# A three-product float32 matmul on one NeuronCore: the high weights times both parts of the input in one product of 512 columns, the two halves added by VectorE

## The chip, the cores and the metric

The kernel runs on one NeuronCore of a Trainium2 chip. The metric is the device time of one execution in microseconds (us). A kernel is timed in several runs, and the median is its time.

## What is computed

Two residual networks are run one behind the other on 256 tokens of 2,048 features. The first has two layers that mix a gated unit over chunks with grouped attention, over the tokens and over 256 context tokens; in its last layer the context is only needed for keys and values. The second has four mixers, each followed by a layer norm: a state-space mixer with a causal convolution ("ssd"), attention with forget gates ("fox"), attention with latent queries and keys ("mla"), and a diagonal recurrence with a gate behind it ("s5"). Cut to what matters, each of them is projections around something small:

```python
proj = h @ w_in[layer]                       # 2,048 x 5,632, first network
x = x + gate * (concat([sgu, attn]) @ w_out[layer])
...
z, xbc, dt = split(h @ ssd_w_in)             # 2,048 x 10,368, then y @ ssd_w_out (4,096 x 2,048)
q, k, v, z, f = split(h @ fox_w_in)          # 2,048 x 8,320,  then y @ fox_w_out
q_lat, kv_lat, k_pe, z = split(h @ mla_w_in) # 2,048 x 3,200,  then two up-projections and y @ mla_w_out
u, z = split(h @ s5_w_in)                    # then y @ s5_w_glu, a sigmoid, and @ s5_w_out
h = layer_norm(ALPHA * h + out)              # behind each mixer of the second network
```

All inputs and the output are float32.

## The kernel before, in words

**Data.** Features lie on the 128 partitions and tokens along the free axis: `xT` is 16 tiles of 128 features by 256 tokens. All weights come as one stream of units of 8 tiles of 128 x 128 (512 KB), in an order that `sequence()` fixes. SyncE loads unit n into `raw[n % 4]` once unit n - 4 has been multiplied (semaphore `multiplied`).

**Precision.** A weight and an input are each kept as two parts in the matmul's reduced float32 type. For a unit of weights ScalarE makes the high part, `w_hi` = a rounded copy of `raw` (`split_hi`, L452), and VectorE the low part, `w_lo` = `raw` - `w_hi` (`split_lo`, L459). For the input of a projection the same is done once, into `act_hi` and `act_lo`. A weight tile then takes three products: `w_hi` x `act_hi` (L513), `w_hi` x `act_lo` (L515) and `w_lo` x `act_hi` (L517), all summed in one PSUM bank. Each product is preceded by its own load of the weights.

**Blocks and slots.** `flow` runs one stage. Its work is a list of blocks; a block is 128 output features, mostly 16 weight tiles (2 units) and so 48 products. In the first network's layer 0 a block has 512 columns (tokens and context), and so have the four blocks of keys and values of layer 1, in two pieces of 256; all others have 256. When all tiles of a block are multiplied, it is taken out of its bank: by ScalarE (an activation, its line is that of a `take_...` function) for the projections into a mixer and for the gate of s5, by VectorE for those out of it (`add_gated` L1651, `add_scaled` L1692: the result goes onto `xT`).

**Order on the engines.** There is no scheduler; each engine runs through the slots g in order. In slot g

- TensorE multiplies block g and then does the mixer's own products that stand in that slot (`tensor_side`: transposes, scores, sums);
- ScalarE makes the high parts up to two units beyond the end of block g (`split_hi(ends[g] + 1 + AHEAD)`, `AHEAD` = 2), does the mixer's steps of the slot (`scalar_early`), waits until block g is multiplied and takes it;
- VectorE makes the low parts up to the same unit, does the mixer's steps of the slot (`vector_side`), and takes block g only if it is a block that VectorE takes.

```python
def scalar(act):
    for g in range(slots):
        split_hi(act, ends[g] + 1 + AHEAD)
        ...
        if taken_by(g, "act"):
            act.wait_ge(multiplied, ends[g] + 1)
            blocks[g].take(act, blocks[g].bank).then_inc(taken["act"], 1)
```

So the high part of the third unit behind block g comes after block g was taken, while the low part of that unit waits for that high part alone.

**Stages.** In this order: the modulation of the first network, the projections into and out of layer 0 and layer 1, ssd in and out, fox in and out, mla in and out, s5 in, the gate of s5, s5 out, the last layer norm. The ssd projections come in eight groups; from the second group on a group has ten blocks, b, c, four x and four z (`ssd_order`). On VectorE a b, c or x block brings three convolution steps in the slot behind it (`add_taps`, L1926), and the group brings a reciprocal, gates, scalings and masks (L1954 to L1996). `norm_root` is a scratch tile of 128 x 256, used by the norms at stage starts.

## Time and profile before

| | us |
|---|---|
| median of 3 runs | 3648.49 |
| lowest and highest | 3647.06, 3650.87 |
| the profiled execution: its own time | 3651.35 |
| the profiled execution: span, first to last instruction | 3649.5 |
| busy: PE, DVE, ACT, POOL | 3413.2, 1960.7, 1845.3, 438.4 |

PE is TensorE, PEld its weight loads, DVE VectorE, ACT ScalarE, POOL GpSimd, SP SyncE. "L459" is line 459 of the kernel before. In a timeline each row has its start in us, its length in us, the engine, the line, the operation, the tiles (out<-in), partitions x elements and, with x, how many were merged; in brackets stands how long the engine was idle before it and what ended that. Busy PE time counts overlapping matmuls as one; how fast matmuls follow each other is read from their starts. The granted clock of TensorE was 0.970 of full speed on average.

### The profile page before, as it was taken

The page shows a single profiled execution, that of the slowest core. Times are in us where ns is not written, and L with a number is a line of the kernel's source. Part 1 is how long each engine was busy: PE and PEld are TensorE (multiplying, and loading weights), DVE is VectorE, ACT ScalarE, POOL GpSimd, SP SyncE. Part 2 cuts the span into 40 slices and gives each one's busy share as a digit, 9 for nine tenths or more (in the row PEclk, how much of TensorE's full clock was granted, in tenths as well). Part 3 has the DMA queues.
Part 4 walks back from the last instruction along what each step waited for, and adds up shares of the span by engine and source line. Part 5 has one row for each costly group of instructions (what it writes and reads, how often), then busy time and mean ns, then how long its engine had stood idle before and what let it go on. Part 6 is the DMA issues. An engine that isn't in the chain of part 4 may idle for free.

```text
span 3649.5 us, 60172 instructions
## 1 busy us (share of the span) xinstructions
PE 3413.2 (94%) x25589; PEld 3067.3 (84%) x25589; DVE 1960.7 (54%) x2698; ACT 1845.3 (51%) x2906; POOL 438.4 (12%) x604
## 2 busy tenths in 40 slices
PE   6899999999899999999999989999989998898897
PEld 2577767778688999999999979999989988788797
DVE  1423322233554455666666465555576556899755
ACT  1334433332456645677675344555455654666443
POOL 0110011101000000000000010000020003787302
PEclk9999999999999999999999989999989999899998
DMA  9654555532233455554554535455544334333353
GB/s 386 216 174 150 173 174 192 196 116 98 75 122 133 168 179 179 177 177 168 193 178 158 183 133 180 168 168 169 169 138 162 129 135 165 116 126 117 114 177 136
DMA packets 157963, 589.83 MB, mean 162 GB/s; under 512 B 18352, under 2 KB 18384, under 8 KB 156032
## 3 DMA queue, kind: packets, MB, share of 16 engines
q1 hardware_dynamic: 135216, 497.64, 39.7%
q0 software_dynamic: 21904, 86.24, 6.8%
q8 instruction: 203, 3.33, 0.4%
q10 hardware_dynamic: 576, 2.10, 0.2%
q14 instruction: 64, 0.52, 0.0%
HBM read 583.69 MB, written 2.21 MB: 161 GB/s over the span
## 4 chain that ended last, share of the span: by engine, by line
PE 75%; DVE 10%; DMA 6%; ACT 5%; issue 3%; POOL 1%; POOLq 0%; DVEq 0%; SPq 0%; ACTq 0%
PE psum_all L513 21%; PE psum_all L517 21%; PE psum_all L515 21%; DMA raw<-in_stream 4%; DMA mod_early<-in_stream 2%; DVE w_lo L459 2%; PE psum_all L725 2%; ACT w_hi L452 1%; DVE s_vd L2906 1%; PE psum_all L1327 1%; PE psum_all L1297 1%; DVE s_vb L2905 1%; ACT ssd_seg L1866 1%; DVE s_im_n L2912 1%; DVE s_im_c L2915 1%
## 5 line engine op out<-in xcount | busy, mean ns | idle before, releaser
L513 PE MATMUL psum_all<-act_hi,w_hi 128*128 128x256 f32 (+1 forms) x6704 | 2059.0, 307 | 85.0 <-DVE act_lo L884 55.5
L515 PE MATMUL psum_all<-act_lo,w_hi 128*128 128x256 f32 (+1 forms) x6704 | 2021.7, 302 | 0.0
L517 PE MATMUL psum_all<-act_hi,w_lo 128*128 128x256 f32 (+1 forms) x6704 | 2020.6, 301 | 0.0
L459 DVE TENSOR_TENSOR w_lo<-raw,w_hi 128x1024 fp32r<-128x1024 f32 x866 | 1070.2, 1244 | 1259.4 <-ACT w_hi L452 1257.4
L513 PEld LDWEIGHTS psum_all<-act_hi,w_hi 128*128 128x128 f32 x6704 | 1296.4, 193 | 182.7 <-issue 101.0
L452 ACT ACTIVATE w_hi<-raw 128x1024 fp32r<-128x1024 f32 x866 | 910.3, 1057 | 849.5 <-DMA raw<-in_stream 848.1
L515 PEld LDWEIGHTS psum_all<-act_lo,w_hi 128*128 128x128 f32 x6704 | 1297.2, 193 | 42.2 <-issue 3.1
L517 PEld LDWEIGHTS psum_all<-act_hi,w_lo 128*128 128x128 f32 x6704 | 1295.4, 193 | 41.7
L699 POOL DMA_DIRECT2D mod_late<-in_stream x128 | 67.7, 533 | 657.5 <-PE psum_all L725 554.9
L952 POOL TENSOR_TENSOR ln_acc<-xT 128x256 f32<-128x256 f32 x8 | 5.9, 735 | 1028.7 <-DVE xT L1692 1028.7
L644 PE MATMUL psum_all<-mod_early,s_silu 128*32 128x512 f32 x256 | 57.8, 645 | 29.0 <-DMA mod_early<-in_stream 28.8
L952 POOL TENSOR_TENSOR ln_acc<-ln_acc,xT 128x256 f32<-128x256 f32 x44 | 47.4, 1077 | 215.0 <-DVE xT L1692 215.0
L1926 DVE SCALAR_TENSOR_TENSOR conv_acc<-conv_x,params,conv_acc 128x255 f32<-128x255 f32 x144 | 69.3, 481 | 3.4
L644 PEld LDWEIGHTS psum_all<-mod_early,s_silu 128*32 128x32 f32 x256 | 9.2, 112 | 72.8 <-DMA mod_early<-in_stream 68.5
L725 PE MATMUL psum_all<-mod_late,small 128*2 128x512 f32 x512 | 67.4, 599 | 0.0
L1651 DVE SCALAR_TENSOR_TENSOR xT<-psum_all,modulation,xT 128x256 f32<-128x256 f32 x32 | 15.4, 482 | 85.2 <-PE psum_all L517 85.1
L1866 ACT ACTIVATE ssd_seg<-ssd_seg,ssd_src 128x128 f32<-128x128 f32 x192 | 58.5, 388 | 2.0 <-DMA ssd_seg<-acs_rows 2.0
L2001 POOL DMA_DIRECT2D acs_rows<-ssd_acs x1 | 0.6, 560 | 480.7 <-DVE ssd_red L1918 480.7
L669 DVE TENSOR_TENSOR modulation<-psum_all,params 128x16 f32<-128x16 f32 x12 | 2.1, 175 | 102.9 <-PE psum_all L660 60.7
L2006 POOL DMA_DIRECT2D ssd_seg<-acs_rows x8 | 4.3, 534 | 437.0 <-PE psum_all L1810 435.2
L980 DVE TENSOR_TENSOR ln_d<-xT,ln_half 128x256 f32<-128x256 f32 (+1 forms) x28 | 43.4, 1548 | 12.4 <-POOLq L441 12.3
L866 ACT ACTIVATE xT<-xT,params 128x256 f32<-128x256 f32 x64 | 34.8, 592 | 29.8 <-DVE xT L1013 28.8
(475 smaller groups left out, 3325.5 us busy)
## 6 DMA issues: line engine op xcount, KB each, us to landing
raw<-in_stream SPq DMA_DIRECT2D x866, 512.0 KB, 3.2
mod_late<-in_stream POOLq DMA_DIRECT2D x128, 512.0 KB, 5.0
mod_early<-in_stream SPq DMA_DIRECT2D x64, 512.0 KB, 8.9
ssd_seg<-acs_rows POOLq DMA_DIRECT2D x8, 1536.0 KB, 6.7
ctxT<-in_ctx SPq DMA_DIRECT2D x2, 2048.0 KB, 13.9
xT<-in_x SPq DMA_DIRECT2D x1, 2048.0 KB, 16.0
fox_key_cum<-cum_rows POOLq DMA_DIRECT2D x1, 2048.0 KB, 8.3
out<-xT SPq DMA_DIRECT2D x4, 512.0 KB, 2.6
```

Of the source, the lines that this page charges most:

```text
L452: act.activation(w_hi[:, n % RING, :], raw[:, n % RING, :], ACT.Copy).then_inc(hi_ready, 1)
L459: dve.tensor_tensor(w_lo[:, n % RING, :], raw[:, n % RING, :], w_hi[:, n % RING, :].bitcast(F32), ALU.subtract).then_inc(lo_ready, 1)
L513: pe.matmul(sums, w_hi[:, n % RING, cols], block.rhs(kk, True, block.width), start=(kk == 0), stop=False)
L515: pe.matmul(sums, w_hi[:, n % RING, cols], block.rhs(kk, False, block.width), start=False, stop=False)
L517: last = pe.matmul(sums, w_lo[:, n % RING, cols], block.rhs(kk, True, block.width), start=False, stop=(kk == block.kt - 1))
L644: last = pe.matmul(bank[rows, :], s_of[:, k, :], units_of[:, m % ring, h * 512:(h + 1) * 512], start=(pair == 0), stop=(pair == PAIRS - 1))
L699: pool.dma_start(late_units[:, m % LATE_RING, :], ins["stream"][u]).then_inc(late_landed[m % LATE_RING], 16)
L725: last = pe.matmul(bank[rows, :], s_late[:, 2 * pair + e, :], late_units[:, m % LATE_RING, h * 512:(h + 1) * 512], start=(pair == 0), stop ...
L952: pool.tensor_tensor(acc, acc if b % 8 > 1 else xT[:, b - 1, :], xT[:, b, :], ALU.add) \
L980: dve.tensor_tensor(self.d[:, a:end, :], xT[:, a:end, :], self.half[:, :].unsqueeze(1).broadcast_to([P, end - a, T]), ALU.subtract) \
L1866: one = act.activation(s, s, ACT.Relu, bias=src_cum[:, g * HG + j, k:k + 1], scale=-1.0)
L1926: dve.scalar_tensor_tensor(out=conv_acc[i % 2][:, back:T], in0=conv_x[i % 2][:, 0:T - back], scalar=conv_col(block, tap), in1=conv_acc[i % ...
```

## The change

The two parts of the input become one tile, `act_parts`, part 0 high and part 1 low. A block may be `wide`: its high weights are then multiplied with both parts in one product of 512 columns (two pieces of 256) into the whole bank, high x high in columns 0 to 255 and high x low in columns 256 to 511; the low weights times the high input (256 columns) go to the first half as before. The halves are added on the way out. For a block that ScalarE takes, VectorE adds them into `norm_root` (`add_halves`, a sum over two), and ScalarE reads that tile in place of the bank; for a block that VectorE takes, a second operation adds the second half. A semaphore `halves_added` carries the first from VectorE to ScalarE, and an addition waits until ScalarE has taken the block before. Wide are: in layer 1 all blocks but those of keys and values, 40; in ssd in 81; in fox in 65; in mla in those whose input is the tokens, 25; in the gate of s5 16; and in the five stages out of a mixer (layer 1, ssd, fox, mla, s5) the blocks 0 to 14, 75 in all. Not wide are layer 0, the last block of every stage out, the up-projections of mla and s5 in. The order in which ssd's second input is kept in the tile changes with it (`result`), and its products take the same operands.

```diff
+HIGH, LOW, BOTH = 0, 1, slice(0, 2)
...
-        act_hi = keep("act_hi", [P, 32 * T], F32R)
-        act_lo = keep("act_lo", [P, 32 * T], F32R)
+        act_parts = keep("act_parts", [P, 2, 32 * T], F32R)
+        act_hi, act_lo = act_parts[:, 0, :], act_parts[:, 1, :]
...
+                    if item.wide and item.taker == "act":
+                        added_at[0] += 1
+                        item.added, item.previous, last_wide[0] = added_at[0], last_wide[0], item
...
-                block.bank = psum[place][:, 0:block.width]
+                block.bank, block.both = psum[place][:, 0:block.width], psum[place].rearrange("p (v t) -> p v t", v=2)
...
-                    pe.matmul(sums, w_hi[:, n % RING, cols], block.rhs(kk, True, block.width),
-                              start=(kk == 0), stop=False)
-                    pe.matmul(sums, w_hi[:, n % RING, cols], block.rhs(kk, False, block.width),
-                              start=False, stop=False)
-                    last = pe.matmul(sums, w_lo[:, n % RING, cols], block.rhs(kk, True, block.width),
+                    if block.wide:
+                        pe.matmul(block.both, w_hi[:, n % RING, cols], block.rhs(kk, BOTH, block.width),
+                                  start=(kk == 0), stop=False)
+                    else:
+                        pe.matmul(sums, w_hi[:, n % RING, cols], block.rhs(kk, HIGH, block.width),
+                                  start=(kk == 0), stop=False)
+                        pe.matmul(sums, w_hi[:, n % RING, cols], block.rhs(kk, LOW, block.width),
+                                  start=False, stop=False)
+                    last = pe.matmul(sums, w_lo[:, n % RING, cols], block.rhs(kk, HIGH, block.width),
                                      start=False, stop=(kk == block.kt - 1))
...
+            def add_halves(dve, block, end):
+                dve.wait_ge(multiplied, end)
+                if block.previous:
+                    dve.wait_ge(taken["act"], block.previous.count)
+                dve.reduce_sum(norm_root[:, :], block.both.rearrange("p v t -> p t v"), AX_X).then_inc(halves_added, 1)
...
                     if taken_by(g, "act"):
-                        act.wait_ge(multiplied, ends[g] + 1)
-                        blocks[g].take(act, blocks[g].bank).then_inc(taken["act"], 1)
+                        if blocks[g].wide:
+                            act.wait_ge(halves_added, blocks[g].added)
+                        else:
+                            act.wait_ge(multiplied, ends[g] + 1)
+                        blocks[g].take(act, norm_root[:, :] if blocks[g].wide else blocks[g].bank).then_inc(taken["act"], 1)
...
+                    if taken_by(g, "act") and blocks[g].wide:
+                        add_halves(dve, blocks[g], ends[g] + 1)
                     if taken_by(g, "dve"):
                         dve.wait_ge(multiplied, ends[g] + 1)
-                        blocks[g].take(dve, blocks[g].bank).then_inc(taken["dve"], 1)
+                        blocks[g].take(dve, blocks[g].both if blocks[g].wide else blocks[g].bank).then_inc(taken["dve"], 1)
...
         def add_scaled(dve, ps, b):
-
-            return dve.scalar_tensor_tensor(out=xT[:, b, :], in0=xT[:, b, :], scalar=ALPHA, in1=ps,
-                                            op0=ALU.mult, op1=ALU.add)
+            if b == KT - 1:
+                return dve.scalar_tensor_tensor(out=xT[:, b, :], in0=xT[:, b, :], scalar=ALPHA, in1=ps,
+                                                op0=ALU.mult, op1=ALU.add)
+            ordered = order["vector"]
+            dve.scalar_tensor_tensor(out=xT[:, b, :], in0=xT[:, b, :], scalar=ALPHA, in1=ps[:, 0, :],
+                                     op0=ALU.mult, op1=ALU.add).then_inc(ordered.sem, 1)
+            dve.wait_ge(ordered.sem, ordered.step())
+            return dve.tensor_tensor(xT[:, b, :], xT[:, b, :], ps[:, 1, :], ALU.add)
```

`add_gated` gets the same second operation as `add_scaled` for the last layer, and the other calls pass `wide=True` for the blocks listed.

**TensorE, in the middle of fox in**, the last two weight tiles of a block and the score product of a head behind it. Before:

```order
L515 MATMUL psum_all<-act_lo,w_hi 128x256
L517 MATMUL psum_all<-act_hi,w_lo 128x256
L513 MATMUL psum_all<-act_hi,w_hi 128x256
L515 MATMUL psum_all<-act_lo,w_hi 128x256
L517 MATMUL psum_all<-act_hi,w_lo 128x256
L2082 MATMUL psum_all<-consts,fox_p_19718 128x128 x3
L2219 MATMUL psum_all<-fox_k,fox_q 128x128
```

Now:

```order
L533 MATMUL psum_all<-act_parts,w_lo 128x256
L526 MATMUL psum_all<-act_parts,w_hi 128x512
L533 MATMUL psum_all<-act_parts,w_lo 128x256
L2130 MATMUL psum_all<-consts,fox_p_17483 128x128 x3
L2267 MATMUL psum_all<-fox_k,fox_q 128x128
```

(L2082, now L2130, turns the probabilities of the head before.) Two products are one, of 512 columns, and the third is as it was. This occurs 5,072 times.

**VectorE, in ssd in**, the slots of the first two x blocks of a group (`add_taps` of the block before, the reciprocal and scalings of the group before, its low part). Before:

```order
L1926 SCALAR_TENSOR_TENSOR conv_acc_11085<-conv_x_11087,params,conv_acc_11085 128x253
L1985 RECIPROCAL ssd_root<-ssd_root 128x256
L1990 SCALAR_TENSOR_TENSOR ssd_z_11075<-ssd_z_11075,params,ssd_root 128x256 x4
L459 TENSOR_TENSOR w_lo<-raw,w_hi 128x1024 x2
L1926 SCALAR_TENSOR_TENSOR conv_acc_11084<-conv_x_11086,params,conv_acc_11084 128x255
L1926 SCALAR_TENSOR_TENSOR conv_acc_11084<-conv_x_11086,params,conv_acc_11084 128x254
L1926 SCALAR_TENSOR_TENSOR conv_acc_11084<-conv_x_11086,params,conv_acc_11084 128x253
L1996 TENSOR_TENSOR act_lo<-ssd_z_11075,act_hi 128x1024
L459 TENSOR_TENSOR w_lo<-raw,w_hi 128x1024 x2
L1926 SCALAR_TENSOR_TENSOR conv_acc_11085<-conv_x_11087,params,conv_acc_11085 128x255
L1926 SCALAR_TENSOR_TENSOR conv_acc_11085<-conv_x_11087,params,conv_acc_11085 128x254
```

Now:

```order
L1972 SCALAR_TENSOR_TENSOR conv_acc_10353<-conv_x_10355,params,conv_acc_10353 128x253
L2031 RECIPROCAL ssd_root<-ssd_root 128x256
L2036 SCALAR_TENSOR_TENSOR ssd_z_10344<-ssd_z_10344,params,ssd_root 128x256 x4
L561 TENSOR_REDUCE norm_root<-psum_all 128x256
L468 TENSOR_TENSOR w_lo<-raw,w_hi 128x1024 x2
L1972 SCALAR_TENSOR_TENSOR conv_acc_10352<-conv_x_10354,params,conv_acc_10352 128x255
L1972 SCALAR_TENSOR_TENSOR conv_acc_10352<-conv_x_10354,params,conv_acc_10352 128x254
L1972 SCALAR_TENSOR_TENSOR conv_acc_10352<-conv_x_10354,params,conv_acc_10352 128x253
L2042 TENSOR_TENSOR act_parts<-ssd_z_10344,act_parts 128x1024
L561 TENSOR_REDUCE norm_root<-psum_all 128x256
L468 TENSOR_TENSOR w_lo<-raw,w_hi 128x1024 x2
L1972 SCALAR_TENSOR_TENSOR conv_acc_10353<-conv_x_10355,params,conv_acc_10353 128x255
```

An addition out of the bank (`norm_root<-psum_all`) stands at the end of each slot, behind the slot's own work and ahead of the next two low parts.

**ScalarE, in the same stage**, the slots of the first two z blocks of a group. Before:

```order
L1866 ACTIVATE ssd_seg<-ssd_seg,ssd_src 128x128 x6
L2024 ACT_TABLE_LOAD
L2024 ACTIVATE ssd_z_11075<-psum_all 128x256
L452 ACTIVATE w_hi<-raw 128x1024 x2
L1857 ACTIVATE ssd_x<-conv_acc_11085 128x256
L1872 ACT_TABLE_LOAD
L1872 ACTIVATE ssd_seg<-ssd_seg 128x1536
L2024 ACT_TABLE_LOAD
L2024 ACTIVATE ssd_z_11075<-psum_all 128x256
L452 ACTIVATE w_hi<-raw 128x1024 x2
```

Now:

```order
L1912 ACTIVATE ssd_seg<-ssd_seg,ssd_src 128x128 x6
L2070 ACT_TABLE_LOAD
L2070 ACTIVATE ssd_z_10343<-norm_root 128x256
L461 ACTIVATE w_hi<-raw 128x1024 x2
L1903 ACTIVATE ssd_x<-conv_acc_10353 128x256
L1918 ACT_TABLE_LOAD
L1918 ACTIVATE ssd_seg<-ssd_seg 128x1536
L2070 ACT_TABLE_LOAD
L2070 ACTIVATE ssd_z_10343<-norm_root 128x256
L461 ACTIVATE w_hi<-raw 128x1024 x2
```

The order is the same, and the two high parts (`w_hi<-raw`) of the next slot come behind a take as before; the take now reads `norm_root`, which VectorE has written in that slot.

## Rows read from the trace of the kernel before

**Rows 1.** The page, part 5: busy us, mean ns, idle before, what ended it
```profile
L459 DVE TENSOR_TENSOR w_lo<-raw,w_hi 128x1024 fp32r<-128x1024 f32 x866 | 1070.2, 1244 | 1259.4 <-ACT w_hi L452 1257.4
```

**Rows 2.** Waits of PE in the whole span: us in total, times, longest
```profile
PE psum_all L513 <- DVE w_lo L459: 13.7, 4, 6.3
PE psum_all L1818 <- ACT ssd_x L1857: 16.3, 8, 2.8
```

**Rows 3.** Timeline of PE, products of 256 columns: start, us, instruction
```profile
1251.20 0.28 PE L513 MATMUL psum_all<-act_hi,w_hi 128*128 128x256 f32 x1
...
1251.92 0.28 PE L513 MATMUL psum_all<-act_hi,w_hi 128*128 128x256 f32 x1
```

**Rows 4.** Timeline of PE, layer 1, products of 512 columns in two pieces
```profile
985.43 0.39 PE L513 MATMUL psum_all<-act_hi,w_hi 128*128 128x512 f32 x1
...
991.55 0.39 PE L513 MATMUL psum_all<-act_hi,w_hi 128*128 128x512 f32 x1
```

**Rows 5.** Groups of VectorE by shape: busy us, mean ns, idle before
```profile
L1692 DVE SCALAR_TENSOR_TENSOR xT<-xT,psum_all 128x256 f32<-128x256 f32 x64 | 26.6, 416 | 10.9 <-PE psum_all L517 10.2
...
L1507 DVE TENSOR_REDUCE head_stat<-psum_all 128x1 f32<-128x512 f32 x32 | 20.5, 685 | 2.1 <-PE psum_all L1299 1.9
```

**Rows 6.** Busy us by stretch: PE, PEld, DVE, ACT, POOL, then clock and DMA
```profile
1741.80:1807.90 66.10, 64.33 (x533) 62.93 (x532) 44.34 (x57) 48.46 (x80) 0.53 (x1) 1.00 0.54 183
2255.00:2299.00 44.00, 44.00 (x364) 43.69 (x363) 23.95 (x39) 23.15 (x38) 0.00 (x0) 1.00 0.50 168
1268.60:1309.30 40.70, 40.70 (x342) 40.70 (x342) 22.56 (x30) 21.07 (x32) 0.00 (x0) 1.00 0.54 182
3441.00:3527.50 86.50, 86.50 (x723) 86.50 (x722) 51.24 (x72) 41.62 (x59) 0.00 (x0) 1.00 0.54 183
2710.00:2750.00 40.00, 39.38 (x315) 38.97 (x314) 32.71 (x74) 25.16 (x38) 0.00 (x0) 0.98 0.50 167
```

**Rows 7.** Timeline of ScalarE: a block is taken, six groups of ten blocks apart
```profile
1537.05 0.56 ACT L2015 ACTIVATE conv_acc<-psum_all,params 128x256 f32<-128x256 f32 x1 [4.66 <-PE psum_all L517]
...
1944.08 0.39 ACT L2024 ACTIVATE ssd_z<-psum_all 128x256 f32<-128x256 f32 x1 [4.46 <-PE psum_all L517]
```

**Rows 8.** Timeline of VectorE in a group of ten blocks
```profile
1754.02 1.52 DVE L1926 SCALAR_TENSOR_TENSOR conv_acc<-conv_x,params,conv_acc 128x255 f32<-128x255 f32 x3
...
1790.99 2.36 DVE L459 TENSOR_TENSOR w_lo<-raw,w_hi 128x1024 fp32r<-128x1024 f32 x2 [2.33 <-ACT w_hi L452]
1793.27 0.42 DVE L1954 TENSOR_TENSOR ssd_z<-ssd_z,ssd_y 128x256 f32<-128x256 f32 x1
```

**Rows 9.** Timeline of ScalarE in the same group
```profile
1754.84 0.56 ACT L2015 ACTIVATE conv_acc<-psum_all,params 128x256 f32<-128x256 f32 x1
...
1755.55 1.06 ACT L452 ACTIVATE w_hi<-raw 128x1024 fp32r<-128x1024 f32 x1
...
1774.59 2.17 ACT L452 ACTIVATE w_hi<-raw 128x1024 fp32r<-128x1024 f32 x2
...
1782.94 0.38 ACT L2024 ACTIVATE ssd_z<-psum_all 128x256 f32<-128x256 f32 x1
1783.22 1.99 ACT L452 ACTIVATE w_hi<-raw 128x1024 fp32r<-128x1024 f32 x2
...
1789.91 2.00 ACT L452 ACTIVATE w_hi<-raw 128x1024 fp32r<-128x1024 f32 x2
```

**Rows 10.** Timelines in the gate of s5: a take on ScalarE, a step on VectorE
```profile
3500.18 0.46 ACT L3026 ACTIVATE s_glu<-psum_all,params 128x256 f32<-128x256 f32 x1
3500.54 1.05 ACT L452 ACTIVATE w_hi<-raw 128x1024 fp32r<-128x1024 f32 x1
...
3500.31 0.42 DVE L2942 TENSOR_TENSOR act_lo<-s_glu,act_hi 128x256 fp32r<-128x256 f32 x1 [0.48 <-ACT act_hi L2864]
```

**Rows 11.** Timeline of VectorE at the start of two stages
```profile
1427.63 2.35 DVE L459 TENSOR_TENSOR w_lo<-raw,w_hi 128x1024 fp32r<-128x1024 f32 x2
...
2199.39 3.46 DVE L459 TENSOR_TENSOR w_lo<-raw,w_hi 128x1024 fp32r<-128x1024 f32 x3
```

More of the change, by code:

```diff
@@ L307 @@
     shape: Any = None
+    wide: bool = False
+    added: int = 0
+    previous: Any = None
 @dataclass
@@ L1649, in take @@
                         dve.wait_ge(ctx_landed, 16)
+                    if last and b < KT - 1:
+                        ordered = order["vector"]
+                        for n in range(2):
+                            one = dve.scalar_tensor_tensor(out=xT[:, b, :], in0=ps[:, n, :],
+                                                           scalar=mod_col(layer, b + 2 * KT, 0), in1=xT[:, b, :],
+                                                           op0=ALU.mult, op1=ALU.add)
+                            if n == 0:
+                                one.then_inc(ordered.sem, 1)
+                                dve.wait_ge(ordered.sem, ordered.step())
+                        return one
                     for n, x in enumerate((xT, ctxT)[:parts]):
@@ L2174, in output_blocks @@
                 return [Block(KT, T, act_rhs(T, first=KT), lambda dve, ps, b=b: add_scaled(dve, ps, b), "dve",
-                              None if b else wait_tile) for b in range(KT)]
+                              None if b else wait_tile, wide=b < KT - 1) for b in range(KT)]
         def keys(tile):
@@ L2322, in fox @@
                 take = take_f if name == "f" else take_z(h) if name == "z" else take_part(parts[name], h)
-                blocks.append(Block(KT, T, act_rhs(T), take, wait=None if blocks else norms[0].wait_tile))
+                blocks.append(Block(KT, T, act_rhs(T), take, wait=None if blocks else norms[0].wait_tile, wide=True))
             blocks = halves_first(blocks, lead) + heads.output_blocks()
@@ L3036, in s5 @@
             blocks += [None]
-            blocks += [Block(KT, T, act_rhs(T, first=KT), take_glu(b), wait=None if b else wait_y) for b in range(KT)]
+            blocks += [Block(KT, T, act_rhs(T, first=KT), take_glu(b), wait=None if b else wait_y, wide=True) for b in range(KT)]
             blocks += [Block(KT, T, act_rhs(T), lambda dve, ps, b=b: add_scaled(dve, ps, b), "dve",
-                             None if b else wait_out) for b in range(KT)]
+                             None if b else wait_out, wide=b < KT - 1) for b in range(KT)]
             norms.append(LayerNorm(3, 4, 5, out=False))
```

51 lines of the change are left out of this document (31 added, 20 removed).

## Prediction

> **What bounds the kernel now.** I began with the busy times: TensorE is busy for 94% of the span, VectorE for 54%, ScalarE for 51%. Such a share is an average, so the waits came next: TensorE waits for low weight parts for 13.7 us in all and for the transposed inputs of ssd for 16.3 us [rows 2]. In nearly every stretch it is the bound. Then its timeline, for the price of a product: six of 256 columns take 1251.92 - 1251.20 = 0.72 us, 0.120 each [rows 3]; 27 of 512 columns, their columns in two pieces of 256 as the change has them, take 6.12 us, 0.2267 each [rows 4]. So two narrow products cost 0.240 and the wide one 0.2267: each product seems to carry about 13 ns besides its columns.
>
> Last, and for this change above all, the two engines that prepare weights. VectorE's low parts leave it idle for 1259.4 us, 1257.4 of these until ScalarE's high part is there [rows 1]. That idle time is the lead of ScalarE over nobody: VectorE is a follower with time to spare. In a group of ten ssd blocks it is busy for 44.3 of 66.1 us, in two heads of fox for 23.95 of 44.0, in fifteen gate blocks for 51.2 of 86.5, at the start of mla for 32.7 of 40.0 [rows 6].
>
> **The change, part by part.**
>
> *TensorE.* A weight tile costs 3 x 0.120 = 0.360 us today and 0.2267 + 0.120 = 0.3467 then: 0.0133 less. Tiles by stage: layer 1 in 40 x 16 = 640, out of the mixers 60 x 16 + 15 x 32 = 1,440, ssd in 1,296, fox in 1,040, mla in 400, the gate 256; in sum 5,072 and 67 us. It counts only where TensorE stays the bound.
>
> The Trainium skill ("TensorE: Matmul & The Clock Gate", Part 1, "Wait — 56ns, not 53.3ns?") puts the fixed cost of a product at full clock at about 2.5 ns. By that the 5,072 removed products would be worth 13 us and not 67. The trace differs: 13 ns per product stand in rows 3 and 4, and the sum goes by them.
>
> *The addition.* VectorE gets 227 sums of two halves out of PSUM. None is in the trace. The nearest row is the reduction of 512 columns out of PSUM, 0.685 us; the lower bound is an operation on 256 columns of PSUM, 0.416 [rows 5]. The upper one, if the jumps between the halves cost a second pass over 512 columns, is 0.685 plus twice the 0.27 by which these two differ, 1.22. I take 0.69, since as many elements are read. For the 75 blocks that VectorE takes, a second operation of 0.42 us is added; VectorE has no more than this to do there, nobody takes the bank sooner than 5.5 us later, and only the last norms see a trace of it: 1 us in all.
>
> *The wait it adds.* Today VectorE's work of a slot and ScalarE's take are independent. Now the take stands behind the addition, the addition behind VectorE's work of the slot, and that behind the low parts of the two units ahead; and behind the take stand ScalarE's next high parts, for which VectorE's next low parts wait. This is a ring, and one turn of it is one block. In it VectorE is idle from the end of its addition to the first low part: 0.04 until ScalarE starts, 0.71 until ScalarE has taken a convolution block and starts a high part (1754.84 to 1755.55) or 0.28 for a z block (1782.94 to 1783.22), and 1.08 until the low part starts (1789.91 to 1790.99) [rows 8, 9]. That is 1.83 or 1.40 us. A stretch can't be shorter than VectorE's own work in it, plus 0.69 and this handover per block.
>
> - *ssd in*, ten blocks: 44.3 + 10 x 0.69 + 6 x 1.83 + 4 x 1.40 = 67.8. In one slot ScalarE is the slower: from a high part at 1774.59 to the take at 1782.94 are 8.35 us, where VectorE needs 1.08 + 2.28 for the pair of low parts + 1.5 for the convolution steps + 0.73 = 5.6 [rows 8, 9]: 2.8 more, 70.6. TensorE's wait for the transposes' inputs, 16.3 / 8 = 2.0 per group today [rows 2], stays, since its release comes from ScalarE in that same stretch: 72.5. Today it is 66.1 [rows 6], and 407.0 / 6 = 67.8 on average over six groups [rows 7]. The difference is 6.4 or 4.7; I take 5.5, so six groups cost 33. The group before them has TensorE's side work of two groups; 3. The end of the stage, 1.
> - *Starts of ssd and fox.* VectorE ends a long chain of small steps and then makes low parts that ScalarE has readied long before (1427.63 and 2199.39 [rows 11]). Now the addition, the take and one high part come first, 0.69 + 0.04 + 0.71 + 1.08 = 2.5, plus 0.7 for the first block's own addition: 3 for fox, and 6 for ssd, whose next block is caught too.
> - *mla's start*: 32.7 + 7 x (0.69 + 1.40) = 47.3 against 40.0 [rows 6]: 7.3 slower. The other 17 wide blocks give back 17 x 16 x 0.0133 = 3.6. Net 3.7.
> - *The gate of s5*: 51.2 + 15 x (0.69 + 0.04 + 0.36 + 1.08) = 83.8, and 0.48 per block for which VectorE waits inside its slot for ScalarE's high part of the input [rows 10]: 91.0 against 86.5 [rows 6]. 4.5 slower, and nothing gained.
> - *fox in*: 23.95 + 7 x 2.09 = 38.6, below 44.0 - 1.5 [rows 6]. The ring is not the bound, and TensorE's gain counts in full: 1,040 x 0.0133 = 13.8. The same holds for layer 1 in, 8.5, whose slots have little work on VectorE, and in the stages out, where ScalarE does not wait: 19.2.
>
> *Sum:* - 8.5 - 19.2 - 13.8 + 33 + 3 + 1 + 6 + 3 + 3.7 + 4.5 + 1 = + 13.7 us. The profiled execution took 3651.35 us, so 3665; the median lies 2.9 lower, so the forecast is **3662 us**. With the clock a little worse or better and the ssd group at its two ends the case itself spans 3645 to 3685. A run of this kernel can tell about 0.2% (7.3 us) from no change.
>
> **Rivals.**
>
> - *The additions are covered.* VectorE is idle for over 1,200 us, and the additions are worth 157. If the lead of two units absorbs the longer path to the take, no stretch becomes longer; this decides if an ssd group comes out at 66 us or less. Then all 67.5 us are gained less the starts (9) and the norms (1): 3651 - 57 - 3 = 3591. For it: ScalarE's high parts also wait for transfers today. Against it: the bound above is a sum over a ring, and a lead does not shorten a ring. 0.10.
> - *The ring binds, but barely.* With additions of 0.42 an ssd group has 67.8 + 2.8 - 2.7 = 67.9 and no further wait: no loss in six groups, mla's start + 5.4, the gate + 0.5: - 41.5 + 10 + 1.8 + 0.5 + 1 = - 28, 3620. 0.13.
> - *The addition is slow.* At 1.22, each turn of a binding ring is 0.53 longer: 70 ssd blocks, 7 of mla, 15 of the gate, 49 us: 3711. 0.09.
> - *The wide product gains nothing.* If the 13 ns come from something that a row of 512 and 256 columns in turn keeps, such as the change between loads of different parts ahead of each product, the 41.5 us of the stages where TensorE is the bound are not gained, and the rest stays: 3662 + 41.5 = 3703. The 0.2267 of rows 4, with a load of its own for each product, speaks against it. 0.03. (By the Trainium skill's 2.5 ns, "TensorE: Matmul & The Clock Gate", 41.5 x 2.5 / 13.3 = 7.8 us of them would remain, and the time would be 3696.)
> - *More of the span at the low clock.* The granted clock is 1.00 in the group of rows 6 and falls where TensorE idles; it will idle for some 9 us more per ssd group. Where the ring binds, a slower product is hidden in it, so I give this no term of its own and let it stand in the upper half of the range.
>
> **How the numbers follow.** The forecast has 0.62, the rivals 0.10, 0.13, 0.09 and 0.03, and 0.03 is left for what I don't see. Faster by over 0.2% (below 3641): 0.10 + 0.13 + 0.02 = 0.25. Within 0.2%: the lower part of the forecast's own range, 0.15. Slower: 0.60. The range is 3615 to 3705: it takes in the barely binding ring and most of what lies above the forecast, and leaves out the covered case and the slow addition, 0.19.
>
> **What would show it.** In the profile after, products of 512 columns should follow one of 256 by 0.120 and be followed after 0.227. The addition should take 0.69. An ssd group should last 71 to 73 us, with VectorE's idle time put down to high parts in pieces of about 1.8 and 1.4 us, and TensorE waiting for low parts for tens of us where today it is 13.7 in all. The fox stretch of 44.0 should last 42.5, fifteen gate blocks about 91. If an ssd group lasts 66 us or less, the argument of the ring is wrong; if fox in isn't about 10 us shorter, the price of the product is.

## The result, and the profile after

| | us |
|---|---|
| before, median of 4 runs | 3647.77 (3644.67 to 3650.87) |
| after, median of 4 runs | 3699.22 (3693.91 to 3713.11) |
| ratio after to before | 1.0145, 95% interval 1.0128 to 1.0162 |
| after, the profiled execution: its own time, its span | 3694.71, 3692.9 |

The change makes the kernel 51 us slower by the medians, and 43.4 by the two profiled executions (3694.71 - 3651.35). Forecast were 13.7. The time lies in the predicted range of 3615 to 3705, on the side that was forecast, but far up in it. The medians are known to a few us only (four runs each, 3693.91 to 3713.11 after), and all that follows by stage is read from one trace of each kernel.

The first view is the timeline of TensorE in layer 1 (start, us, instruction), the answer to [rows 3, 4]:

```profile
1249.72 0.40 PE L526 MATMUL psum_all<-act_parts,w_hi 128*128 128x512 f32 x1
1249.95 0.28 PE L533 MATMUL psum_all<-act_parts,w_lo 128*128 128x256 f32 x1
1250.07 0.40 PE L526 MATMUL psum_all<-act_parts,w_hi 128*128 128x512 f32 x1
...
1252.19 0.40 PE L526 MATMUL psum_all<-act_parts,w_hi 128*128 128x512 f32 x1
```

From 1249.72 to 1252.19 there are seven weight tiles: 0.353 each, where the sum of [rows 3] and [rows 4] promised 0.3467 and before had 0.360. Half of the gain per tile isn't there. The other half of the bill is on VectorE and ScalarE. Groups of VectorE (busy us, mean ns, idle before, what ended it), the answer to [rows 1]:

```profile
L468 DVE TENSOR_TENSOR w_lo<-raw,w_hi 128x1024 fp32r<-128x1024 f32 x866 | 1066.4, 1247 | 1109.9 <-ACT w_hi L461 1108.6
L561 DVE TENSOR_REDUCE norm_root<-psum_all 128x256 f32<-128x512 f32 x227 | 155.7, 686 | 29.3 <-PE psum_all L533 28.1
```

The addition takes 0.686, as forecast, and VectorE still idles for over 1,100 us. But its consumer waits. Waits of TensorE and of ScalarE (us in total, times, longest), the answer to [rows 2]:

```profile
PE psum_all L526 <- DVE w_lo L468: 31.1, 21, 9.5
PE psum_all L1871 <- ACT ssd_c L1903: 29.3, 7, 5.1
PE psum_all L1864 <- ACT ssd_x L1903: 20.4, 8, 3.4
```

```profile
ACT conv_acc L2061 <- DVE norm_root L561: 125.9, 46, 9.9
ACT ssd_z L2070 <- DVE norm_root L561: 61.7, 18, 5.3
```

The last two rows are new: 188 us in which ScalarE stands before a take of ssd until VectorE has added the halves. Before, it stood 62 us at the same takes, until TensorE had multiplied the block:

```profile
ACT conv_acc L2015 <- PE psum_all L517: 41.1, 16, 5.3
ACT ssd_z L2024 <- PE psum_all L517: 21.3, 15, 4.5
```

TensorE's waits for low parts rise from 13.7 to 31.1, and it now waits for the inputs that ScalarE makes from the taken blocks more than before: ssd_c 29.3 and ssd_x 20.4, where it was 3.5 and 16.3.

One turn of the ring of an ssd block, VectorE first and then ScalarE:

```profile
1565.66 0.68 DVE L561 TENSOR_REDUCE norm_root<-psum_all 128x256 f32<-128x512 f32 x1
1568.27 2.36 DVE L468 TENSOR_TENSOR w_lo<-raw,w_hi 128x1024 fp32r<-128x1024 f32 x2 [1.93 <-ACT w_hi L461]
1570.54 1.52 DVE L1972 SCALAR_TENSOR_TENSOR conv_acc<-conv_x,params,conv_acc 128x255 f32<-128x255 f32 x3
1571.98 0.55 DVE L2027 TENSOR_TENSOR ssd_cb<-psum_all,consts 128x384 f32<-128x384 f32 x1
1572.45 0.68 DVE L561 TENSOR_REDUCE norm_root<-psum_all 128x256 f32<-128x512 f32 x1
```

```profile
1566.38 0.60 ACT L2061 ACTIVATE conv_acc<-norm_root,params 128x256 f32<-128x256 f32 x1 [1.98 <-DVE norm_root L561]
1566.88 0.40 ACT L2063 ACTIVATE conv_x<-norm_root 128x256 f32<-128x256 f32 x1
1567.19 2.00 ACT L461 ACTIVATE w_hi<-raw 128x1024 fp32r<-128x1024 f32 x2
```

The addition ends at 1566.34, ScalarE takes at 1566.38 and makes a high part at 1567.19, and VectorE's low parts start at 1568.27: a handover of 1.93 in which VectorE does nothing. The forecast had 1.83. The turn lasts 6.79 us, while TensorE needs 16 x 0.353 = 5.65 for the block, besides the mixer's own products. The same kind of take ten blocks apart, at ScalarE:

```profile
1541.90 0.60 ACT L2061 ACTIVATE conv_acc<-norm_root,params 128x256 f32<-128x256 f32 x1 [5.43 <-DVE norm_root L561]
...
1615.69 0.60 ACT L2061 ACTIVATE conv_acc<-norm_root,params 128x256 f32<-128x256 f32 x1 [5.34 <-DVE norm_root L561]
```

This group takes 73.8 us, and the four behind it, by the same take, 73.2 to 75.0. Forecast were 72.5, the average of before was 67.8 [rows 7]. Stretches with busy us of PE, PEld, DVE, ACT and POOL, then granted clock, DMA share and GB/s: all of ssd in, the start of mla, the two heads of fox, the gate [rows 6]:

```profile
1401.40:2006.50 605.10, 537.72 (x3007) 459.36 (x3007) 407.48 (x552) 389.73 (x643) 4.82 (x9) 0.94 0.48 162
...
2739.40:2794.10 54.70, 44.14 (x218) 36.70 (x217) 39.08 (x81) 25.71 (x39) 0.00 (x0) 0.91 0.38 125
2294.98:2338.25 43.27, 43.27 (x251) 37.78 (x251) 28.21 (x46) 23.33 (x37) 0.00 (x0) 1.00 0.52 170
3477.60:3568.50 90.90, 86.93 (x481) 73.05 (x479) 58.89 (x87) 42.20 (x59) 0.00 (x0) 1.00 0.52 174
```

VectorE's two rows within ssd in show that the ring is closed there (busy us, mean ns, idle before):

```profile
L468 DVE TENSOR_TENSOR w_lo<-raw,w_hi 128x1024 fp32r<-128x1024 f32 x163 | 194.2, 1223 | 179.8 <-ACT w_hi L461 179.7
...
L561 DVE TENSOR_REDUCE norm_root<-psum_all 128x256 f32<-128x512 f32 x80 | 54.7, 684 | 10.2 <-PE psum_all L533 10.0
```

Its work (407.5 us), its waits for ScalarE's high parts (179.7) and its waits for TensorE (10.0) make 597 of the 605 us: VectorE waits for ScalarE or works, and hardly ever waits for TensorE. What TensorE waits for in this stage are mostly ssd_c and ssd_x, 49.7 us; low parts are 14.1 (8.4 before). The loop holds TensorE up through the inputs of the mixer's own products, and not, as forecast, mainly through low parts.

And ssd in before, in the same view of stretches:

```profile
1403.20:1963.20 560.00, 528.62 (x4305) 516.37 (x4305) 360.97 (x473) 387.78 (x644) 4.83 (x9) 0.98 0.51 176
```

By stage, from the last product of the stage before to its own last one, in the profiled executions (us). The kernels on the right are those of the next section: no additions, wide only where unbound (so narrow in ssd in, mla in and the gate), the later take, the later take but not in layer 1.

| stage | before | after | forecast | measured | no add. | unbound | later | later 2 |
|---|---|---|---|---|---|---|---|---|
| layer 1 in | 357.9 | 356.9 | -8.5 | -1.0 | 356.4 | 356.5 | 393.6 | 358.2 |
| ssd in | 560.0 | 605.1 | +43 | +45.1 | 554.1 | 554.3 | 579.6 | 581.1 |
| fox in | 437.9 | 431.4 | -10.8 | -6.5 | 428.6 | 431.9 | 428.8 | 429.9 |
| mla in | 308.2 | 318.1 | +3.7 | +9.9 | 304.8 | 307.4 | 313.6 | 314.5 |
| the gate | 118.3 | 121.7 | +4.5 | +3.4 | 115.6 | 115.7 | 114.6 | 114.1 |
| five stages out | 566.9 | 562.1 | -18.2 | -4.8 | 552.5 | 555.1 | 557.8 | 557.3 |

Stages without a wide product and what lies behind the last stage moved by -2.8 in sum. Together that is the + 43.4, within rounding.

How far a stage scatters can be read from experiments 1 and 2, which are the changed kernel with rows of products behind its last stage. Ahead of these rows their traces give, beside the column "after": layer 1 in 355.1 and 355.5, ssd in 609.5 and 609.3, fox in 431.3 and 431.9, mla in 320.2 and 319.7, the gate 121.3 and 120.0, the stages out 556.7 and 560.3. Differences of 2 to 5 us in a stage show little.

### The profile page after: what moved, and what is told of

Read it like the earlier page. It is cut to its first block, busy times and chain, and to the rows that moved or that the text cites. A ratio compares the mean times of both kernels' runs of the same rounds, so it can differ in the third digit from the quotient of the medians.

```text
span 3692.9 us, 50550 instructions
## 1 busy us (share of the span) xinstructions
PE 3401.5 (92%) x20517; PEld 2807.4 (76%) x20517; DVE 2129.6 (58%) x3000; ACT 1846.6 (50%) x2906; POOL 448.9 (12%) x604
## 4 chain that ended last, share of the span: by engine, by line
PE 63%; DVE 16%; ACT 9%; DMA 6%; issue 4%; POOL 1%; POOLq 0%; DVEq 0%; SPq 0%; ACTq 0%
PE psum_all L526 21%; PE psum_all L533 17%; PE psum_all L529 7%; PE psum_all L531 7%; DVE w_lo L468 5%; DMA raw<-in_stream 4%; ACT w_hi L461 4%; DMA mod_early<-in_stream 2%; PE psum_all L752 2%; DVE norm_root L561 1%; PE psum_all L1324 1%; PE psum_all L1354 1%; DVE s_vd L2954 1%; DVE s_im_n L2960 1%; DVE s_vb L2953 1%
## 5 line engine op out<-in xcount | busy, mean ns | idle before, releaser
L533 PE MATMUL psum_all<-act_parts,w_lo 128*128 128x256 f32 (+1 forms) x6704 | 2015.0, 301 | 0.0
L526 PE MATMUL psum_all<-act_parts,w_hi 128*128 128x512 f32 x5072 | 1846.6, 407 | 64.3 <-DVE w_lo L468 31.1
L533 PEld LDWEIGHTS psum_all<-act_parts,w_lo 128*128 128x128 f32 x6704 | 1290.4, 192 | 45.5 <-issue 2.9
L461 ACT ACTIVATE w_hi<-raw 128x1024 fp32r<-128x1024 f32 x866 | 899.1, 1052 | 621.4 <-DMA raw<-in_stream 620.4
L526 PEld LDWEIGHTS psum_all<-act_parts,w_hi 128*128 128x128 f32 x5072 | 971.0, 191 | 312.6 <-issue 51.5
L529 PE MATMUL psum_all<-act_parts,w_hi 128*128 128x512 f32 (+1 forms) x1632 | 593.2, 363 | 40.2 <-DVE act_parts L911 32.6
L531 PE MATMUL psum_all<-act_parts,w_hi 128*128 128x512 f32 (+1 forms) x1632 | 577.3, 354 | 0.0
L529 PEld LDWEIGHTS psum_all<-act_parts,w_hi 128*128 128x128 f32 x1632 | 313.8, 192 | 127.7 <-issue 69.4
L531 PEld LDWEIGHTS psum_all<-act_parts,w_hi 128*128 128x128 f32 x1632 | 314.3, 193 | 38.4 <-issue 0.5
L561 DVE TENSOR_REDUCE norm_root<-psum_all 128x256 f32<-128x512 f32 x227 | 155.7, 686 | 29.3 <-PE psum_all L533 28.1
L2061 ACT ACTIVATE conv_acc<-norm_root,params 128x256 f32<-128x256 f32 x48 | 28.8, 601 | 125.9 <-DVE norm_root L561 125.9
```

Source lines behind the costliest of these rows:

```text
L461: act.activation(w_hi[:, n % RING, :], raw[:, n % RING, :], ACT.Copy).then_inc(hi_ready, 1)
L526: pe.matmul(block.both, w_hi[:, n % RING, cols], block.rhs(kk, BOTH, block.width), start=(kk == 0), stop=False)
L529: pe.matmul(sums, w_hi[:, n % RING, cols], block.rhs(kk, HIGH, block.width), start=(kk == 0), stop=False)
L531: pe.matmul(sums, w_hi[:, n % RING, cols], block.rhs(kk, LOW, block.width), start=False, stop=False)
L533: last = pe.matmul(sums, w_lo[:, n % RING, cols], block.rhs(kk, HIGH, block.width), start=False, stop=(kk == block.kt - 1))
L561: dve.reduce_sum(norm_root[:, :], block.both.rearrange("p v t -> p t v"), AX_X).then_inc(halves_added, 1)
```

## The experiments

Two explanations had to be told apart: the ring, which costs where it binds, and the price of the wide product, which gives less than it should everywhere. Each got a test that leaves the other alone. Every kernel was timed next to the kernel before, whose median was 3647.6 to 3650.2 us each time; a ratio is to that.

**1. The price by itself (e1_rows).** Behind the last stage, rows of products with a weight load each, whose results are used nowhere:

```
...
+            for t in range(64):
+                product(halves, hi(t), x(t, BOTH))
+                product(one[:, 0:T], lo(t), x(t))
...
```

and six others in the same manner.

> The kernel after, and behind its last stage seven rows of products, each with its own weight load, VectorE, ScalarE and the stream idle: three of 256 columns per tile; 512 in two pieces and 256 in turn (the change); 512 in one piece and 256; 512 in two pieces and 256 into another bank; 512 in two pieces alone; 512 in one piece alone; 512 in two pieces and twice 256. Start to start at full clock. In the changed kernel the pair takes 0.235 + 0.117 = 0.352 to 0.356 us, not 0.3467. Theory 'the mixed row keeps it': three of 256 take 0.360, the pair 0.352 to 0.356 here too, two pieces or one, and 512 alone 0.227 per product. Rival 'traffic of the other engines': the pair comes down to 0.347 or less here, where they are idle. Rival 'pieces': the row of one piece takes 0.347 and that of two pieces 0.354. Rival 'the same bank written twice running': only the row with another bank takes 0.347.

The timeline of TensorE. The pair in turn runs from the first row to the second (64 tiles), the one whose 512 columns are in one piece to the third, the one into another bank to the fourth, 128 products of 512 columns in two pieces alone to the fifth:

```profile
3734.82 0.40 PE L3112 MATMUL psum_all<-act_parts,w_hi 128*128 128x512 f32 x1
...
3757.43 0.40 PE L3112 MATMUL psum_all<-act_parts,w_hi 128*128 128x512 f32 x1
...
3780.05 0.40 PE L3112 MATMUL psum_all<-act_parts,w_hi 128*128 128x512 f32 x1
...
3802.66 0.40 PE L3112 MATMUL psum_all<-act_parts,w_hi 128*128 128x512 f32 x1
...
3831.70 0.39 PE L3112 MATMUL psum_all<-act_parts,w_hi 128*128 128x512 f32 x1
```

22.61 / 64 = 0.3533 per tile, and the same for the other two; 29.04 / 128 = 0.2269 for a product of 512 alone, 0.2267 once the row is under way, as in [rows 4]. Three products of 256 took 0.360 per tile. So neither the two pieces, nor the bank, nor the traffic of the other engines matters: all were idle here. A product of 512 and one of 256 in turn cost 0.0067 more than each in a row of its own.

The seventh row has one product of 512 and then two of 256 for each tile. From the start of its first tile to that of its last, 63 tiles later:

```profile
3860.71 0.39 PE L3112 MATMUL psum_all<-act_parts,w_hi 128*128 128x512 f32 x1
...
3890.14 0.39 PE L3112 MATMUL psum_all<-act_parts,w_hi 128*128 128x512 f32 x1
```

That is 29.43 / 63 = 0.467 per tile, and 0.2267 + 2 x 0.120 is 0.4667: here there is no extra. So the theory of the mixed row holds for one narrow product behind each wide one, as the change has it, and not for every row that mixes the two widths.

**2. Is it the change of width? (e5_rows_grouped)** The same rows, with 1, 2, 4 and 8 wide products running and then as many narrow ones.

> The kernel after with rows of products behind its last stage again. In the first such run a tile took 0.360 us in three products of 256, 0.3533 in 512 and 256 in turn, and 512 alone 0.2267 each: 0.0067 more than the sum of the two. Theory 'the change of width costs it': 1, 2, 4 and 8 wide products, then as many narrow ones, take 0.3533, 0.3500, 0.3483 and 0.3475 us per tile. Rival 'it comes with each product of low weights, or each change of its inputs': 0.3533 for all four. Further rows: 384 columns alone 0.120 + 128 x 0.4167 ns = 0.1733; 384 and 256 in turn 0.1733 + 0.120 + 0.003 to 0.007; 128 alone 0.067 if the fixed cost stays 13 ns; 512 and 128 in turn 0.293 and 0.007 to 0.020 if the extra grows with the difference in width.

Where runs of 2, of 4 and of 8 begin, and where the last ends:

```profile
3757.62 0.64 PE L3112 MATMUL psum_all<-act_parts,w_hi 128*128 128x512 f32 x2
...
3779.93 0.63 PE L3112 MATMUL psum_all<-act_parts,w_hi 128*128 128x512 f32 x2
...
3802.38 0.63 PE L3112 MATMUL psum_all<-act_parts,w_hi 128*128 128x512 f32 x2
...
3824.73 0.52 PE L3112 MATMUL psum_all<-act_parts,w_hi 128*128 128x384 f32 x2
```

Per tile 0.3486, 0.3508 and 0.3492 us, after 0.3533 in single turns. It falls, so the product of low weights isn't what costs; but it doesn't fall in the order expected (0.3500, 0.3483, 0.3475): runs of 4 are dearer than runs of 2. The extra per turn is 7, 4, 16 and 20 ns for 1, 2, 4 and 8. A fixed price per change of width is therefore wrong too, as the seventh row above had shown. The 384 columns took 0.1733, as expected, and 384 and 256 in turn 0.2933, the plain sum: no extra at all. A product of 128 took 0.112 and not 0.067; 512 and 128 in turn 0.340, 1.6 ns over the sum, where 7 to 20 were expected. What makes the extra of 512 and 256 in turn stays open.

**3. The ring taken away (e2_no_addition).**

```
-                    if taken_by(g, "act") and blocks[g].wide:
-                        add_halves(dve, blocks[g], ends[g] + 1)
...
+                        act.wait_ge(multiplied, ends[g] + 1)
+                        blocks[g].take(act, blocks[g].bank).then_inc(taken["act"], 1)
```

> Leaves out the 227 additions: ScalarE takes the first half of the bank, so the product of high weights and low inputs is not added in there. VectorE's 156 us of additions and ScalarE's wait for them go. Theory 'ring': ssd in, mla in and the gate, 45.1, 9.9 and 3.4 us longer than before, fall back to before's length or by up to 5, 1 and 1 us below it, so the whole takes 3628 to 3640. Rival 'the products themselves are slower there' (two pieces, the bank written twice, the layout of the parts): ssd in stays over 590 us and the whole over 3675.

3615.39 us, 0.9905 of before (0.9887 to 0.9924), 13 us below the expected range. ssd in takes 554.1 us, mla in 304.8, the gate 115.6, and the granted clock of ssd in is back at 0.97 without anything done for it:

```profile
1404.40:1958.40 554.00, 521.17 (x3008) 447.98 (x3009) 359.21 (x472) 388.47 (x643) 4.83 (x9) 0.97 0.53 177
```

So the low clock in the changed kernel comes with the additions and isn't a cause beside them; for the same products TensorE is busy 537.7 us with them and 521.2 without.

The run also measures what the wide products give in the whole kernel: 3649.09 - 3615.39 = 33.7 us, and 5,072 tiles x 0.00667 = 33.8. Where TensorE is the bound all through and at the full clock, it shows to the hundredth: the two heads of fox take 43.27 us and the fifteen gate blocks 84.8, where before 44.01 and 86.4 less 0.0067 per tile are 43.26 and 84.8. By stage the sum doesn't come out so well. In ssd in the price would be 8.6 us, and the stage takes 554.1, just what it takes with narrow products in the three kernels of experiment 8 (554.3, 553.5, 554.5). Why these are about 6 us shorter than the one trace of the kernel before isn't known, and so the agreement in the sum may in part be luck.

And the run gives what the additions cost in all: 3699.22 - 3615.39 = 84 us. The forecast's own terms say 13.7 + 67.5 = 81, but with a gain of 0.0133 per tile; with half of that, the gain given up in ssd in, mla in and the gate is 11.2 and not 22.4 us, and the same terms say 70. The 81 is near the 84 by luck.

**4. The ring made longer (e7_addition_twice).** Each addition of ssd in is made twice.

```
+                if block.place is not None:
+                    dve.reduce_sum(norm_root[:, :], block.both.rearrange("p v t -> p t v"), AX_X).then_inc(order["vector"].sem, 1)
+                    dve.wait_ge(order["vector"].sem, order["vector"].step())
                 dve.reduce_sum(norm_root[:, :], block.both.rearrange("p v t -> p t v"), AX_X).then_inc(halves_added, 1)
```

> The change, with each addition of ssd in made twice, one after the other (81 more of 0.69 us, 56 us of VectorE, which is idle for over 1,100). Theory 'ring': 70 of them lie in stretches where it binds, so ssd in becomes 70 x 0.69 = 48 us longer (40 to 56), 649, and the whole 3740 to 3755. Rival 'the loss is one of the low clock or of TensorE's own waits, the ring has slack': ssd in grows by less than 20 and the whole stays under 3720.

3737.15 us (ratio 1.0242, 1.0226 to 1.0258), 38 more than the change, and ssd in is 641.3 us, 36 longer. VectorE in ssd in, the added group and what is left of its idle time:

```profile
L468 DVE TENSOR_TENSOR w_lo<-raw,w_hi 128x1024 fp32r<-128x1024 f32 x161 | 191.1, 1222 | 160.7 <-ACT w_hi L461 160.7
...
L564 DVE TENSOR_REDUCE norm_root<-psum_all 128x256 f32<-128x512 f32 x80 | 55.3, 691 | 2.8
L562 DVE TENSOR_REDUCE norm_root<-psum_all 128x256 f32<-128x512 f32 x80 | 54.7, 683 | 9.2 <-PE psum_all L533 9.1
```

An engine that idles for 180 us in this stage is given 55 us more, and the stage grows by 36 (by 32 against the two other traces of the changed kernel, 609). If each addition counts in full where the ring binds, that is about 47 to 53 of the 80, not the 70 counted, and stage and whole end a little below what was expected. The rival, under 20 us, is out.

**5. The ring opened at ScalarE (e4_take_later).** ScalarE makes the high parts of the next slot first and takes the block behind them.

```
                 for g in range(slots):
                     split_hi(act, ends[g] + 1 + AHEAD)
+                    if g and taken_by(g - 1, "act") and blocks[g - 1].wide:
+                        take_wide(g - 1)
...
```

> All products and additions as in the change, but ScalarE takes a wide block only after the high parts of the next slot, so that these no longer stand behind VectorE's addition. Theory 'the handover binds, not the work': VectorE's own work of an ssd group is 44.3 + 6.9 = 51 us, far below 66, so ssd in comes down to 550 to 568 us, mla in to 300 to 310, and the whole to 3630 to 3650. Rival 'VectorE has too much work, or the low clock costs it': ssd in stays above 590 and the whole above 3680.

The whole missed: 3692.49 us (ratio 1.0123, 1.0101 to 1.0146), the same as the change. By stages it is two effects. ssd in falls from 605.1 to 579.6, mla in from 318.1 to 313.6, the gate from 121.7 to 114.6; for ssd in and mla in that is less than expected (550 to 568, 300 to 310), but the rival's 590 is out. And layer 1 in grows from 356.9 to 393.6. TensorE's waits in the attention of layer 1, in this kernel:

```profile
PE psum_all L1357 <- DVE q L1515: 18.6, 6, 3.4
...
PE psum_all L1383 <- ACT vg_t L1467: 8.8, 8, 1.3
```

In the change these two rows are 7.7 and 1.7, so they account for 18 of the 37 us; TensorE is also busy 15 us longer in that stage, at a granted clock of 0.93 in place of 0.97. A take that stands behind a high part stands behind that part's transfer too: ScalarE waits 137.9 us for weights there, 29.1 in the change. In ssd in about half of the loss is left; of TensorE's waits, 23.5 us are for ssd_x and 11.9 for ssd_c, both made from taken blocks, and 1.5 for a bank.

**6. What was left in ssd (e9_later_bank_free).** The later take everywhere but in layer 1, and a bank is free once it is added up.

```
+                if block.before and tiles[0] == 0 and block.before.wide and block.before.taker == "act":
+                    pe.wait_ge(halves_added, block.before.added)
```

> All products and additions of the change; the take after the next high parts in ssd in, fox in, mla in and the gate, but not in layer 1 (whose stage it made 37 us longer); and TensorE may write a bank again once the addition has read it, without waiting for the take. From 3692.5 of the kernel with the later take everywhere: 37 less, 3655. Theory 'what is left of ssd's loss are its own inputs, made later because the take is later' (TensorE waited 23.5 and 11.9 us there for ssd_x and ssd_c, 1.5 for a bank): ssd in stays 572 to 578 us. Rival 'TensorE waits for the bank': ssd in falls to 555 to 562 and the whole to 3640.

3656.54 us (ratio 1.0023, 1.0013 to 1.0034), as expected, and ssd in 581.1, 3 above its expected range: the bank is not what it waits for. The waits of TensorE in that stage name the inputs, as before:

```profile
PE psum_all L1872 <- ACT ssd_x L1911: 27.5, 8, 4.5
PE psum_all L1879 <- ACT ssd_c L1911: 11.5, 6, 2.2
```

That the inputs are late because the take is late fits these rows; a version with them made earlier wasn't tried.

**7. The groups of eight in the kernel (e6_grouped).** All wide products of a unit, then all its narrow ones.

```
+                        for weights, ready in ((w_hi, hi_ready), (w_lo, lo_ready)):
+                            pe.wait_ge(ready, n + 1)
+                            for kk in here:
...
```

> The whole change, but with the eight wide products of a unit first and then its eight products of low weights, for which alone the low parts are waited. Theory 'width change': 5.8 ns per tile where TensorE is the bound (3,120 tiles, 18 us), the ring as in the change: 3699 - 18 = 3681, ssd in still 595 to 603 us. Rival 'TensorE's wait for low parts costs ssd, not the ring': the low parts are needed 1.8 us later, ssd in falls under 580 and the whole under 3660. Rival 'no price for the change of width': 3695 or more.

3705.76 us (ratio 1.0159, 1.0144 to 1.0174) where 3681 was expected: nothing gained, and ssd in is 608.0. The rival "TensorE's own wait for low parts costs ssd" is out: these parts were needed 8 x 0.23 = 1.8 us later and nothing moved. The 4 ns per tile of the rows above don't show in the whole. Fox in is 3.1 us shorter than in the change (431.4 to 428.3), against 1,040 x 0.0041 = 4.3, but the last stage out is 2.2 longer.

**8. Better versions.** Wide products only where nothing binds (e3_only_where_unbound; in the edit, the flag is gone from the blocks of ssd in, mla in and the gate):

```
-                                    place=len(blocks) % 2, wide=True))
+                                    place=len(blocks) % 2, wide=False))
```

> The wide product only in layer 1 in, fox in and the stages out; ssd in, mla in and the gate as before. Theory 'the loss lies in the three stages where the ring binds': 3694.7 - 45.1 - 9.9 - 3.4 = 3636, ratio 0.996 to before, and ssd in 560 us again. Rival 'a mechanism outside these stages' (the layout of the parts, the second operations): over 3650.

3626.8 us, ratio 0.994 (0.9922 to 0.9959): faster than before by 0.6% and 9 us below what was expected. The traced execution, 3619.88, is the fastest of the six, so its stages may look a little short; ssd in takes 554.3, not 560. With the gate wide as well, and the later take there and in fox in, first in groups of eight (e8_combined), then in turn (e10_best_ungrouped); the edits are those above, and a flag `later` on the blocks of these two stages:

> Wide products in layer 1 in, fox in, the gate and the stages out, in groups of eight as in the run above; ssd in and mla in as before; ScalarE's take after the next high parts in fox in and the gate alone. From 3626.8 of the kernel with wide products only where nothing binds: 3,120 tiles x 5.8 ns = 18 us less, and 3 of fox in's later take: 3606, ratio 0.988. If the change of width has no price in the kernel: 3620 or more. The gate, with its own wide products and the ring broken, takes 87 to 89 us.

> Wide products in layer 1 in, fox in, the gate and the stages out, in turn with the narrow ones as in the change; ssd in and mla in as before; the later take in fox in and the gate. If groups of eight gave nothing: 3620 to 3624, as the combined kernel (3622.0). If the 4.1 ns per tile of the rows (0.3533 against 0.3492) count in the 3,120 tiles: 13 us more than that, 3635. Against the kernel with wide products only where nothing binds (3626.8): 3 us less for fox in, 1 for the gate.

3622.04 (0.9926, 0.9911 to 0.9941) and 3620.87 us (0.9924, 0.991 to 0.9938). So grouping is worth nothing here, and the expectation that took the price of the rows over into the kernel was 16 us too low. The gate takes 117.2 us in the last one, against 118.3 before but 115.7 in the kernel that keeps it narrow; over the four kernels with wide products and the later take it is 114.1 to 117.2, so no gain there can be told from the scatter. Fox in takes 429.8 against 437.9. The last version beats both kernels, by 29 us (0.8%) and by about 78. It keeps ssd in narrow: even without additions that stage took 554.1 with wide products and 554.3 without.

## Why the prediction was right in its sign and too low in its size

- **"Each product seems to carry about 13 ns besides its columns", and so 0.0133 per tile.** This step failed, at the point where two rows of one width each were added up into a row of both. In turn they cost 0.3533, not 0.3467; 0.0067 per tile is the gain. In the stages where TensorE is the bound, 3,120 tiles lose 20.8 us of the 41.5 forecast, and mla's give-back 1.8 of 3.6. 13.7 + 22.6 = 36.3: most of the distance to 43.4. The rival that a mixed row keeps the 13 ns had named the right place and was half true: it keeps half. Its mechanism, a cost of changing between the two, isn't shown (the row with two narrow products has no extra). It was put at 0.03 on the ground that rows 4 have a load for each product, but those rows hold one width. (The Trainium skill's 2.5 ns, "TensorE: Matmul & The Clock Gate", Part 1, "Wait — 56ns, not 53.3ns?", would give an estimated 13 us for 5,072 products; experiment 3 measures 33.7.)
- **The addition, 0.69.** Measured 0.686. Right.
- **The ring in ssd, 72.5 per group, + 43 for the stage with its start and end.** 73.2 to 75.0 and + 45.1; the handover 1.93 for 1.83. The mechanism is right, and tried from three sides: without it 554.1, with a longer one 641.3, opened on one side 579.6. The sum is right by two errors that cancel: five full groups average 74.2 now and 67.6 before, so six cost about 40 and not 33, and start and end of the stage cost about 5 and not 10. What opening the ring leaves, 20 to 25 us, is put down to inputs made late because the take is late, which is argued and not tried.
- **mla's start, + 7.3.** The stretch took 40.0 us before [rows 6] and takes 54.7 now; counted to the same product as now, it was 41.0 before. The forecast's bound was VectorE's work and handovers alone. Work with six additions is 39.1 us now and the six handovers are 1.43 each, as forecast (1.40); what was left out is VectorE waiting inside its slots, 6.2 us: 2.03 for the first high part, 0.55 and 0.81 for act_parts, 0.35 and 0.37 for s5c_step and mla_root, and 2.09 for TensorE. The first three stand in the trace of before as well (2.02, 0.55 and 0.81) and could have been counted. 13.7 instead of 7.3: mis-sized by 6.4, and with the 36.3 this makes 42.7 of the 43.4. That it closes so well is partly luck: stage by stage the price alone doesn't give the differences (layer 1 in gained 1.0 us where 4.3 would be expected of it), and the medians lie 51 us apart, 8 more than the traced executions.
- **The gate, 91.0.** 90.9. Right, and here the waits inside the slot had been counted.
- **Fox in, 42.5 for the two heads, and "if fox in isn't about 10 us shorter, the price of the product is" wrong.** 43.27, which is the 44.0 less 112 tiles x 0.0067 = 0.75, and fox in 6.5 us shorter. The ring didn't bind in that stretch, as said, and the test named in advance pointed at the right term.
- **The stages out, - 19.2.** - 4.8. With the true price they should give 9.6; two of them, the first and the last, show 3.4 us of TensorE at the low clock that they didn't have before. In the two kernels with rows, which are the same up to there, they give 10.2 and 6.6, and in the kernel without additions 14.4. The 9.6 lies within that scatter, which isn't explained further here.
- **What would show it.** TensorE was to wait for low parts "for tens of us": 31.1 in all, but only 14.1 of them in ssd in, where the loss is. That sign was wrong in its place; the waits are for ssd_c and ssd_x.
- **The rivals.** "Covered" would need 3591; even without any addition the kernel takes 3615. "Slow addition" (3711) and "the wide product gains nothing" (3703) lie nearest to the 3699; the first for a reason that the 0.686 rules out, the second for one that is half true.

## What to carry over

Additions on an engine that was busy for 54% of its time cost 84 us, because they made ScalarE wait for VectorE, which waits for ScalarE already: ask not how busy the engine is, but which loop of waits the new operation closes, and add up one turn of it. A price taken from rows of equal instructions holds for rows of equal instructions; measure the mixture in which the change will use it, in a row of some 64 behind the last stage, before summing it over 5,000. And a change that has stages of both signs is best taken stage by stage: here the wide product in the stages with TensorE as the bound alone is worth 0.6%, and 0.8% in the best version.

## What was not expected of the hardware

- A product of 512 columns and one of 256, each with its own weight load, take 0.3533 us in turn, and 0.2267 and 0.120 in rows of their own; 384 and 256 in turn take 0.2933, the plain sum of 0.1733 and 0.120, and one of 512 with two of 256 behind it takes 0.467, the plain sum too.
- Runs of 2, 4 and 8 products of 512 and as many of 256 take 0.3486, 0.3508 and 0.3492 per tile, not in order.
- A product of 128 columns takes 0.112 in a row, as against 0.120 for one of 256: below 256 columns the time hardly falls with the width. Its load is the nearest suspect; the rows don't settle it.
